# Narrow stationary operands dealt over four column groups of the PE array in a diffusion trunk with three kinds of token mixer

## What is computed

```python
sc = jax.nn.silu(c)                                   # (1, 1024), latent tokens
scc = jax.nn.silu(c_ctx)                              # (1024,), context tokens
for l in range(DEPTH):
    mod_p = (scc @ w_mod[l] + b_mod[l])[None, None, :]    # 1024 x 3072, two rows in all
    mod_s = (sc @ w_mod[l] + b_mod[l])[:, None, :]
    hp, gp = _modulate(yp, norm_g[l], mod_p)              # rmsnorm * (1 + scale) + shift, gate
    hs, gs = _modulate(ys, norm_g[l], mod_s)
    ...
# mLSTM: two gates x two directions x four heads, 16 columns
ipre = jnp.einsum('btc,dch->dbht', gin, w_ig) + b_ig[:, None, :, None]
lf = jax.nn.log_sigmoid(jnp.einsum('btc,dch->dbht', gin, w_fg) + b_fg[:, None, :, None])
# GLA: a decay of rank 16, for each of two directions
la = jax.nn.log_sigmoid((h @ w_a1[d]) @ w_a2[d] + b_a[d]) / B_TAU
```

## Time and profile before

| | us |
|---|---|
| runs | 1951.94, 1952.37, 1946.57 (median 1951.94) |
| span of the profiled execution | 1948.8 |
| PE busy | 1816.9 |
| VectorE (DVE) busy | 604.2 |
| ScalarE (ACT) busy | 495.2 |
| GpSimd (POOL) busy | 167.7 |

### The profile page before, as it was taken

One profiled execution on the slowest core, in us unless ns is written; L12 is line 12 of the kernel. 1 busy time (PEld: TensorE's weight loads), 2 busy tenths in 40 slices (PEclk: granted clock), 3 DMA queues, 4 the chain that ended last, 5 costly groups with the idle time before them and its releaser, 6 DMA issues.

```text
span 1948.8 us, 16614 instructions
## 1 busy us (share of the span) xinstructions
PE 1816.9 (93%) x6421; PEld 1050.9 (54%) x6421; DVE 604.2 (31%) x979; ACT 495.2 (25%) x960; POOL 167.7 (9%) x158
## 2 busy tenths in 40 slices
PE   6899999999989899988989998999799998898998
PEld 3355534755655554546455455545455536575655
DVE  0333005336340202375320552321433005445420
ACT  2201323323320114343111222231201223433300
POOL 1000001001000000052043000000100001100100
PEclk9999998999999998999999997999899999999999
DMA  6522222233242321242365221323222221212122
GB/s 189 203 86 86 88 74 76 76 112 116 83 146 95 113 86 43 76 150 98 130 126 156 86 86 44 98 98 110 73 86 87 99 74 44 83 48 87 44 88 75
DMA packets 105140, 185.98 MB, mean 95 GB/s; under 512 B 5136, under 2 KB 54704, under 8 KB 105072
## 3 DMA queue, kind: packets, MB, share of 16 engines
q1 hardware_dynamic: 95816, 158.40, 24.2%
q0 software_dynamic: 8640, 26.46, 4.6%
q10 hardware_dynamic: 616, 0.16, 0.1%
HBM read 164.47 MB, written 20.54 MB: 95 GB/s over the span
## 4 chain that ended last, share of the span: by engine, by line
PE 88%; DVE 5%; ACT 3%; issue 1%; DMA 1%; SPq 0%; DVEq 0%; ACTq 0%; POOLq 0%
PE acc L500 69%; PE mix L500 17%; PE acc L565 1%; DMA out_new_C<-cst 1%; DVE hT L1523 1%; ACT cp L1276 1%; DVE mix L1344 1%; DVE rd L1505 1%; DVE cstat L1666 1%; PE mix L915 0%; DMA ring<-in_a_w_out 0%; DMA cst<-in_c_k_g 0%; DVE dx L1590 0%; DVE hT L1348 0%; DVE fqk L1626 0%
## 5 line engine op out<-in xcount | busy, mean ns | idle before, releaser
L500 PE MATMUL acc<-hT,ring 128*128 128x385 f32 x1664 | 548.3, 491 | 15.8 <-DVE hT L1351 14.4
L500 PEld LDWEIGHTS acc<-hT,ring 128*128 128x128 f32 x1664 | 317.9, 192 | 244.6 <-issue 21.9
L500 PE MATMUL acc<-z,ring 128*128 128x385 f32 x512 | 169.5, 492 | 6.1 <-DMA ring<-in_a_w_out 4.2
L500 PE MATMUL acc<-ring,sc 128*2 128x384 f32 x512 | 170.2, 486 | 1.6 <-ACT mst L992 1.2
L500 PEld LDWEIGHTS acc<-z,ring 128*128 128x128 f32 x512 | 97.9, 192 | 77.7 <-issue 6.1
L500 PE MATMUL mix<-qs,ring 128*128 128x256 f32 x512 | 117.6, 392 | 9.6 <-DVE qs L1507 9.6
L500 PEld LDWEIGHTS mix<-qs,ring 128*128 128x128 f32 x512 | 100.1, 197 | 27.6 <-issue 13.2
L500 PEld LDWEIGHTS acc<-ring,sc 128*2 128x2 f32 x512 | 41.3, 85 | 119.1 <-issue 112.2
L1363 DVE SCALAR_TENSOR_TENSOR y<-acc,modv,y 128x128 f32 x64 | 23.4, 413 | 223.8 <-PE acc L500 223.8
L500 PE MATMUL acc<-ring,hT 128*128 128x512 f32 x192 | 85.5, 608 | 0.0
L500 PE MATMUL acc<-xc,bd 128*128 128x385 f32 x128 | 57.5, 574 | 14.2 <-DVE hT L1523 8.4
(11 more groups left out here) (297 smaller groups left out, 2212.6 us busy)
## 6 DMA issues: line engine op xcount, KB each, us to landing
ring<-in_w_mod SPq DMA_DIRECT2D x64, 768.0 KB, 6.2
ring<-in_a_w_in SPq DMA_DIRECT2D x32, 1024.0 KB, 6.9
ring<-in_state_mlstm_C SPq DMA_DIRECT2D x16, 1024.0 KB, 7.8
out_new_C<-cst POOLq DMA_DIRECT2D x32, 512.0 KB, 3.2
ring<-in_a_w_out SPq DMA_DIRECT2D x16, 1024.0 KB, 7.8
ring<-in_c_w_in SPq DMA_DIRECT2D x16, 1024.0 KB, 7.6
ring<-in_b_w_in SPq DMA_DIRECT2D x12, 1024.0 KB, 6.3
ring<-in_b_w_out SPq DMA_DIRECT2D x4, 1024.0 KB, 6.2
```

The costliest lines, as they stand in the source:

```text
L500: return nc.tensor.matmul(out, lhsT=lhsT, rhs=rhs, start=start, stop=stop)
```

## The change

GROUP = 32 and GROUPS = 4. `column_groups` replaces `group` for the narrow products: matmul n of a product goes to array columns (and PSUM partitions) 32 (n mod 4) and on. Each group starts its sum with its own first matmul and ends it with its last, so that four partial sums of the same rows stand on partitions 0, 32, 64 and 96 on. The next matmul, which contracts over all 128 partitions, adds them.

- *Modulation.* The stationary operand is a window of 32 columns of `sc` (widened to 46 columns, zeroed by DVE first; ACT's fill waits for `sc_zeroed`), so that all 32 rows of a group are written. `mst` has 128 rows. `mod_columns` multiplies `mst` by `gather` (128 x 2, the sum of the identity's four blocks, made once by DVE) where it transposed before.
- *Gate.* Matmul f goes to group f mod 4. The first four, one in each group, have 32-column windows of `gfold`, which write all rows; the halves of `gfold` are swapped for it. `grow` and `gsel` have 128 rows, and four copies make `gsel` instead of one.
- *la.* Windows of 32 columns of `ga1` (16 columns longer, zeroed). `gha` and `ga2` have 128 rows, `ga2` is zeroed and loaded into four places. POOL waits for `ga_zeroed` before its loads, of which there are seven instead of five.

```diff
+GROUP = 32
+GROUPS = P // GROUP
...
-        sc = sb("sc", 2 * KD)
+        sc = sb("sc", 2 * KD + GROUP - 2)
+        gather = sb("gather", 2)
...
-        mst = sb("mst", 2 * MC, rows=2)
+        mst = sb("mst", 2 * MC)
...
-            ga1 = sb("ga1", KD * 2 * RANK, stack=st)
-            ga2 = sb("ga2", 2 * BH * BDK, rows=RANK, stack=st)
-            gha = sb("gha", 2 * W, rows=RANK, stack=st)
+            ga1 = sb("ga1", KD * 2 * RANK + GROUP - RANK, stack=st)
+            ga2 = sb("ga2", 2 * BH * BDK, stack=st)
+            gha = sb("gha", 2 * W, stack=st)
...
             def mod_columns(l, n):
+
                 t = tile(f"modrow{n}", l)
                 moved(pe, t)
-                transposes(tile(f"modcol{n}", l), [
-                    (lambda ps, e=e: ps[:, 2 * e:2 * e + 2], mst[:, seg(n % 2 * MC + e * P, P)])
-                    for e in range(MC // P)])
+                ps = bank(tile(f"modcol{n}", l))
+                pe.wait_ge(gather_ready, 1)
+                for e in range(MC // P):
+                    ins = mm(ps[:, 2 * e:2 * e + 2], mst[:, seg(n % 2 * MC + e * P, P)], gather[:, :], True, True)
+                ins.then_inc(acc_ready, 1)
+
+            def column_groups(ps, pairs):
+
+                for n, (a, b) in enumerate(pairs):
+                    g = GROUP * (n % GROUPS)
+                    ins = mm(ps[g:g + a.shape[1], :], a, b, n < GROUPS, n >= len(pairs) - GROUPS)
+                return ins
...
-                group(ps[0:2, 0:MC], [(sc[:, 2 * k:2 * k + 2], w3[:, k, :]) for k in range(KD)]
-                      ).then_inc(acc_ready, 1)
+                column_groups(ps[:, 0:MC], [(sc[:, seg(2 * k, GROUP)], w3[:, k, :]) for k in range(KD)]
+                              ).then_inc(acc_ready, 1)
...
-                pairs = [(g4[:, f, 1, :], xm3[:, f, 1:1 + W]) for f in range(AT_)]
-                pairs += [(g4[:, f, 0, :], xc3[:, f, :]) for f in range(AT_)]
+                pairs = [(gfold[:, seg(32 * f, 32 if f < GROUPS else 16)], xm3[:, f, 1:1 + W]) for f in range(AT_)]
+                pairs += [(g4[:, f, 1, :], xc3[:, f, :]) for f in range(AT_)]
...
-                    ins = mm(ps[0:16, 0:W], a, b, n == 0, n == len(pairs) - 1)
+                    g = GROUP * (n % GROUPS)
+                    ins = mm(ps[g:g + a.shape[1], 0:W], a, b, n < GROUPS, n >= len(pairs) - GROUPS)
...
-                pe.wait_ge(b_in, 16 * 5)
-                for d in range(2):
-                    group(bank(tile("la", l, d))[0:RANK, 0:W], [(ga14[:, k, d, :], h3[:, k, :]) for k in range(KD)]
-                          ).then_inc(acc_ready, 1)
+                pe.wait_ge(b_in, 16 * 7)
+                for d in range(2):
+                    column_groups(bank(tile("la", l, d))[:, 0:W], [
+                        (ga1[:, seg((2 * k + d) * RANK, GROUP)], h3[:, k, :]) for k in range(KD)]).then_inc(acc_ready, 1)
...
-                move(tile(f"modrow{n}", l), mst[:, seg(n % 2 * MC, MC)], lambda ps: ps[0:2, 0:MC])
+                move(tile(f"modrow{n}", l), mst[:, seg(n % 2 * MC, MC)], lambda ps: ps[:, 0:MC])
...
-                nc.scalar.copy(grow[:, 0:P], ps[0:16, 0:P])
-                move(tile("gate", l, 0), grow[:, P:TC], lambda ps: ps[0:16, LAT:W])
+                nc.scalar.copy(grow[:, 0:P], ps[:, 0:P])
+                move(tile("gate", l, 0), grow[:, P:TC], lambda ps: ps[:, LAT:W])
...
+            nc.vector.memset(sc, 0.0).then_inc(sc_zeroed, 1)
+
+            dve.wait_ge(const_made, CONSTS)
+            nc.vector.tensor_reduce(gather, ident.rearrange("p (g r) -> p r g", r=GROUP)[:, 0:2, :], AX, ALU.add
+                                    ).then_inc(gather_ready, 1)
...
-                nc.vector.tensor_copy(gsel.rearrange("p (n c) -> p n c", c=32)[:, :, 0:AH],
-                                      ident[0:16, 0:16].rearrange("p (n c) -> p n c", c=AH)).then_inc(gsel_ready, 1)
+                for g in range(0, P, GROUP):
+                    ins = nc.vector.tensor_copy(gsel[g:g + 16, :].rearrange("p (n c) -> p n c", c=32)[:, :, 0:AH],
+                                                ident[g:g + 16, g:g + 16].rearrange("p (n c) -> p n c", c=AH))
+                ins.then_inc(gsel_ready, 1)
...
+                nc.vector.memset(ga1[:, KD * 2 * RANK:], 0.0)
+                nc.vector.memset(ga2, 0.0).then_inc(ga_zeroed, 1)
...
             def gla(l):
                 done_before(pool, l - 1)
-                for d in range(2):
-                    pool.dma_start(ga14[:, :, d, :], i["b_w_a1"][0, d].rearrange("(k p) n -> p k n", p=P)).then_inc(b_in, 16)
-                    pool.dma_start(ga2[:, seg(d * BH * BDK, BH * BDK)], i["b_w_a2"][0, d]).then_inc(b_in, 16)
+                pool.wait_ge(ga_zeroed, 1)
+                for d in range(2):
+                    pool.dma_start(ga14[:, :, d, :], i["b_w_a1"][0, d].rearrange("(k p) n -> p k n", p=P)
+                                   ).then_inc(b_in, 16)
+                for g in range(0, P, GROUP):
+                    pool.dma_start(ga2[g:g + RANK, :].rearrange("r (d n) -> r d n", d=2),
+                                   i["b_w_a2"][0].rearrange("d r n -> r d n")).then_inc(b_in, 16)
                 pool.dma_start(gs03, i["state_gla_S"][0, 0].rearrange("d h k v -> k (d h) v")).then_inc(b_in, 16)
```

More of the change, by code:

```diff
@@ L192, in trunk @@
         gfold = kw[0]
-        grow = kw[1][0:16, 0:TC]
-        gsel = kw[1][0:16, TC:TC + P]
+        grow = kw[1][:, 0:TC]
+        gsel = kw[1][:, TC:TC + P]
         vrow = cst[0][:, 0:4 * P]
@@ L229, in trunk @@
             gmask = sb("gmask", LEVELS * P, I32, stack=st)
-            ga1 = sb("ga1", KD * 2 * RANK, stack=st)
-            ga2 = sb("ga2", 2 * BH * BDK, rows=RANK, stack=st)
-            gha = sb("gha", 2 * W, rows=RANK, stack=st)
+            ga1 = sb("ga1", KD * 2 * RANK + GROUP - RANK, stack=st)
+            ga2 = sb("ga2", 2 * BH * BDK, stack=st)
+            gha = sb("gha", 2 * W, stack=st)
         gq3, gk3, gv3, gr3 = v3(gq, BH, TC), v3(gk, BH, TC), v3(gv, NT, D), v3(gr, KD)
         gb4 = gb.rearrange("p (d h t) -> p d h t", d=2, h=BH)
-        ga14 = ga1.rearrange("p (k d n) -> p k d n", k=KD, d=2)
+        ga14 = ga1[:, 0:KD * 2 * RANK].rearrange("p (k d n) -> p k d n", k=KD, d=2)
         gs03, kft3 = v3(gs0, 2 * BH, BDV), v3(kft, 2 * BH, P)
@@ L311, in trunk @@
         b_in, gmask_ready = sem("b_in"), sem("gmask_ready")
+        ga_zeroed = sem("ga_zeroed")
+        gather_ready, sc_zeroed = sem("gather_ready"), sem("sc_zeroed")
         xla_ready = sem("xla_ready")
@@ L1018, in _ @@
             move(tile("vec", 0, 0), vec[:, :])
-            move(tile("vec", 0, 1), sc.rearrange("p (k r) -> p r k", r=2),
+            act.wait_ge(sc_zeroed, 1)
+            move(tile("vec", 0, 1), sc[:, 0:2 * KD].rearrange("p (k r) -> p r k", r=2),
                  lambda ps: ps[:, V_CTX - 2 * P:V_CTX - 2 * P + 16].rearrange("p (r k) -> p r k", r=2), ACT.Silu)
@@ L1178, in gla @@
                 for d in range(2):
-                    move(tile("la", l, d), gha[:, d * W:(d + 1) * W], lambda ps: ps[0:RANK, 0:W])
+                    move(tile("la", l, d), gha[:, d * W:(d + 1) * W], lambda ps: ps[:, 0:W])
                 for n in range(2 * BH):
@@ L1397, in prepare @@
                     t = tile(f"fold{x}", l, m)
-                    g_ = g4[:, :, m // 2, :]
+                    g_ = g4[:, :, 1 - m // 2, :]
                     out = g_ if x == 0 and m != 1 else rd[n % 2][:, 0:256].rearrange("p (f n) -> p f n", n=16)
```

## The result

The changed kernel takes 1828.62 us (median of four runs, 1826.47 to 1832.7) beside 1951.2 for the kernel before: a ratio of 0.938, 95% interval 0.9362 to 0.9397. The prediction was 1834, range 1815 to 1885. The span of the profiled execution went from 1948.8 to 1825.9 us, by 122.9.

What follows compares the result with a forecast made beforehand. TensorE was taken to bound the kernel (busy 93% of the span). Terms -19 - 26 - 2.5 - 5 - 27 - 31 - 7.6 = -118 bring the span from 1948.8 to 1831, plus 3.1 gives 1834 us; range 1815 to 1885.

Steps and rivals of the forecast that it cites:

- Full overlap, 0.76: All dealt products: four column groups of 32 run side by side as two do, giving 1834 us; chance 0.76.
- A part: One modulation part, 16 passes: 1.6 instead of 5.3 us, -3.7, before the gather's added cost.
- the stagger of 0.3: Modulation part: the four groups' starts, set apart by their weight loads, add 0.3 us to 1.29 us.
- the net -3.35: Each modulation part: -3.7 us from overlap, +0.35 us for the gather matmuls, range -3.1 to -3.6.
- The opening: Opening, 8 parts: ring refills limit the gain to 4 us a pair for three pairs, 6.7 the first: -19 us.
- GLA's level loop: Six parts in the loop: PE already waits for DVE, so only -2.5 us, from -6 to +4.
- their old pace: Sign to look for: GLA levels keep their pace, with longer waits for DVE; no size given.
- The loads on POOL: GLA weight loads wait for two DVE memsets, go out from about 684, hidden before `la` at 722: no cost.
- which keep their length: Eight `ga2` tiles behind `la`: ACT sets their pace, so their length does not change.
- Two at a time: Passes start in program order, so only neighbouring groups overlap: -74.5 us, 1877 us; chance 0.14.
- No overlap: Passes of 32-column groups run one by one, only the gather is added: +9 us, 1961 us; chance 0.04.
- draining: Each change of column group drains the array, 0.09 us a change: +32 us, 1984 us; chance 0.06.

Runs made afterwards that it cites:

- the runs with two and one: Changed kernel with two column groups of 32 instead of four: 1865.73 us; changed kernel with the modulation parts alone in one group of 32 columns: 1919.07 us.
- The changed kernel's second trace: The changed kernel itself, unedited, measured again in the same job as the second run of another opening order: 1825.73 us.

## Why the prediction was right

- **The overlap, and its evidence.** The one place with two heads' values side by side carried over to four groups of 32: no group slows another (the runs with two and one). "Full overlap, 0.76" was the case that came. But those rows could not show how long a block may be: head 15's passes start at 1329.39, right behind ACT's copy of their operand (done at 1329.34), when only two passes of head 14 have not started. The prediction doesn't ask that question; dealing in turn kept clear of a limit that was found only afterwards, with blocks of 16 passes.
- **A part.** Predicted 1.6 us, measured 1.43 to 1.48 to the next start: the stagger of 0.3 was too much, and the four loads lie within 0.13 us. The gather costs 0.42, not 0.35. The errors nearly cancel: heads and natten gained 3.3 a part (26.4 / 8), as the net -3.35.
- **The opening.** -18.8 for -19, and PE does wait for the ring, 7.9 us in all. That the sum fits to 0.2 us is luck. From pair to pair the gains are 7.8, 4.9, 5.4 and 0.8 us, where the prediction had 6.7 and three times 4; the last pair lost its gain to the long wait and to the clock behind it. The changed kernel's second trace, with other waits, has -20.8.
- **GLA's level loop.** PE waits longer, as said: 17.9 us before the levels' matmuls instead of 6.3. But the levels don't all keep "their old pace": three of the waits, two of which the profile doesn't put down to DVE or any other engine, cost clock. Timeline of PE in the changed kernel, a level behind a long wait and one behind a short one:

```profile
794.24 4.52 PE L505 MATMUL mix<-fqk 128*128 128x128 f32 x24 [5.06 <-issue]
...
802.38 2.94 PE L505 MATMUL mix<-fqk 128*128 128x128 f32 x24 [1.44 <-DVE fqk L1652]
```

  After 5.06 us of idle time the same 24 passes take 4.52 us instead of 2.94, at a granted clock of 0.62 instead of 1.00; in the three levels behind waits of 5 us and more 6.3 us go that way. The term allowed for it as an end of its range ("if the idle PE loses clock"), and -2.7 came for -2.5.
- **The loads on POOL.** Timeline of POOL in the changed kernel [beside rows 13]:

```profile
620.91 1.80 POOL L1798 DMA_DIRECT2D ga<-in_b_w_a  x2 [134.41 <-DVE ga L1574]
```

  They wait for DVE's memset and go out from 620.91 on; the last, `gs`, has landed by 631.1. Timeline of PE:

```profile
659.37 2.79 PE L505 MATMUL acc<-hT,ga 128*32 128x385 f32 x32
```

  `la` starts at 659.37 with no wait: covered.
- **What was missed.** The step "which keep their length" for the tiles behind `la`: they and the next linear gained 4.3 us, at a granted clock of 1.00 instead of 0.72 and 0.70. It is most of the difference between 1831 and the span of 1825.9. The sum was right to 5 us with one term missing; 2.8 of the 4.3 are shown to come from the rows of `gha` and `ga2`.
- **Rivals.** Two at a time falls by the part's 1.50 us. No overlap and draining fall with it: groups change at every matmul, with no gap between the sets of four loads. On the last, the Trainium skill ("TensorEngine Tiling (Array Packing)", Key Properties) says that tiles work in parallel and that only a change of mode drains; the parts' 1.50 us agree.

## What to carry to other kernels

A narrow stationary operand cost PE the same pass as a full one here (about 0.32 us with 2, 16, 32 and 128 columns), and dealing it over four column groups gave close to a quarter of the time (5.25 to 1.43 us), if the next matmul can add the partial sums. Deal in turn: in blocks of 16 passes most of the overlap was lost. Then read each place for what is late next (here a ring, a DVE chain, a state's write), and before moving work into a gap, ask what chain it covers where it stands.

## What the runs showed of the hardware

- Passes of different column groups overlap fully and may start out of program order, with blocks of four passes for free and blocks of 16 mostly serial (1.5 us for 16 passes; 17.1 for 64, which take 20.9 in one group and 5.4 dealt in turn).
- Eight tiles that contract over 16 rows ran at, and were followed by, a granted clock of 0.70 to 0.80 (two traces), the same tiles with 112 rows of zeros added of 1.00 (eleven traces).
- Of 416 writes of 512 KB, none took over 3.83 us without a 16 KB instruction load inside it; with one they took 3.19 to 5.57 us.
